# Zero-padded keys and values, so that the score and output matmuls of both attentions use all 128 rows and columns

## The reference

```
# first: 16 query heads, 4 key heads, window keys and context keys side by side
s = concat(einsum(q, k_window), einsum(q, k_context), sink)     # 256 + 256 keys
p = softmax(s * 64 ** -0.5 with band mask)
o = einsum(p, v)                                                # head size 64
# second (256 tokens): 8 heads with three branches, then 8 heads with one
for head in 8 "NSA" heads:   # keys of a group are shared by 4 heads
    o = g0 * attn(q, 15 compressed keys) + g1 * attn(q, k_sel) + g2 * attn(q, k_win)
for head in 8 "MoBA" heads:
    o = attn(q, k, causal)
```

## Time and profile before

| | us |
|---|---|
| median of 3 runs | 2453.49 (2449.99 to 2455.32) |
| the profiled execution | 2460.38 |
| its span, first to last instruction | 2459.1 |
| TensorE busy in the span | 2312.9 (94%) |
| VectorE, ScalarE, GpSimd busy | 1482.0, 1067.9, 120.2 |
| mean granted TensorE clock | 0.936 |

### The profile page before, as it was taken

One profiled execution on the slowest core, in us unless ns is written; L12 is line 12 of the kernel. 1 busy time (PEld: TensorE's weight loads), 2 busy tenths in 40 slices (PEclk: granted clock), 3 DMA queues, 4 the chain that ended last, 5 costly groups with the idle time before them and its releaser, 6 DMA issues. The chain is left out here.

```text
span 2459.1 us, 35571 instructions
## 1 busy us (share of the span) xinstructions
PE 2312.9 (94%) x14610; PEld 2030.3 (83%) x14610; DVE 1482.0 (60%) x2461; ACT 1067.9 (43%) x1740; POOL 120.2 (5%) x83
## 2 busy tenths in 40 slices
PE   5999999999899999999999988969996999999998
PEld 3988889998898888998888985569996975588998
DVE  4765775667566677565677565535654554455555
ACT  4522225644652223563222454554544444334444
POOL 1000001100200000110000020010000010000000
PEclk9999999999899999999999987989997995589999
DMA  6545554455354555444555442014655420034553
GB/s 269 189 159 201 186 162 166 149 194 182 112 184 163 199 181 169 162 158 169 181 198 176 158 159 86 1 52 162 234 187 183 155 103 18 1 102 145 186 174 135
DMA packets 70781, 378.21 MB, mean 154 GB/s; under 512 B 7486, under 2 KB 12478, under 8 KB 43994
## 3 DMA queue, kind: packets, MB, share of 16 engines
q1 hardware_dynamic: 67824, 369.91, 43.5%
q10 hardware_dynamic: 2794, 6.02, 0.7%
HBM read 374.85 MB, written 1.05 MB: 153 GB/s over the span
## 5 line engine op out<-in xcount | busy, mean ns | idle before, releaser
L487 PE MATMUL ps_g<-h,w_hi 128*128 128x256 f32 (+1 forms) x4288 | 1003.9, 329 | 13.7 <-DVE h L930 9.4
L842 DVE TENSOR_TENSOR w_lo<-w_raw,w_hi 128x1024 fp32r<-128x1024 f32 (+2 forms) x614 | 689.1, 1124 | 462.3 <-ACT w_hi L1355 461.6
L1355 ACT ACTIVATE w_hi<-w_raw 128x1024 fp32r<-128x1024 f32 (+2 forms) x614 | 592.6, 969 | 627.7 <-PE ps_g L487 522.2
L487 PEld LDWEIGHTS ps_g<-h,w_hi 128*128 128x128 f32 x4288 | 729.3, 192 | 88.5 <-issue 13.8
L487 PE MATMUL ps_g<-h,w_lo 128*128 128x256 f32 (+1 forms) x2144 | 703.0, 328 | 0.0
L487 PE MATMUL ps_g<-hid,w_hi 128*128 128x256 f32 (+1 forms) x2368 | 497.9, 309 | 3.0 <-DVE y L985 2.0
L487 PEld LDWEIGHTS ps_g<-h,w_lo 128*128 128x128 f32 x2144 | 412.3, 192 | 35.5
L487 PEld LDWEIGHTS ps_g<-hid,w_hi 128*128 128x128 f32 x2368 | 388.0, 193 | 26.4 <-DVE w_lo L842 2.5
L487 PE MATMUL ps_g<-hid,w_lo 128*128 128x256 f32 (+1 forms) x1184 | 364.1, 307 | 0.0
L487 PE MATMUL ps_g<-b_h,w_hi 128*128 128x256 f32 x1504 | 276.8, 287 | 8.1 <-DVE b_h L930 7.8
L487 PEld LDWEIGHTS ps_g<-b_h,w_hi 128*128 128x128 f32 x1504 | 236.8, 193 | 11.4 <-issue 9.9
(11 more groups left out here) (245 smaller groups left out, 1857.1 us busy)
## 6 DMA issues: line engine op xcount, KB each, us to landing
w_raw<-in_gu SPq DMA_DIRECT2D x130, 1024.0 KB, 4.9
mod_raw<-in_w_mod SPq DMA_DIRECT2D x128, 512.0 KB, 3.7
w_raw<-in_conv_cu SPq DMA_DIRECT2D x16, 1024.0 KB, 4.8
w_raw<-in_dn00b SPq DMA_DIRECT2D x16, 768.0 KB, 4.2
w_raw<-in_dn01b SPq DMA_DIRECT2D x16, 768.0 KB, 4.2
w_raw<-in_dn10b SPq DMA_DIRECT2D x16, 768.0 KB, 4.2
w_raw<-in_conv_out SPq DMA_DIRECT2D x8, 1024.0 KB, 4.9
w_raw<-in_w_in_a SPq DMA_DIRECT2D x8, 1024.0 KB, 4.8
```

Of the source, the lines that this page charges most:

```text
L487: mm = pe.matmul(at, w[wp][:, k, m * P:(m + 1) * P], acts[ap][:, k, cs], start=(k == 0 and n == 0 and not (one_bank and m)), stop=(k == kc ...
L842: dve.tensor_tensor(w_lo[u % 2][:, cols], w_raw[u % 2][:, cols], w_hi[u % 2][:, cols].bitcast(F32), ALU.subtract).then_inc(lo_made, 1)
L1355: act.activation(w_hi[u % 2][:, cols], w_raw[u % 2][:, cols], ACT.Copy).then_inc(hi_made, 1)
```

## The change

The keys of each head get a tile of their own, with zeros in the other head's 64 rows; the values of each head get 128 columns, with zeros in the other head's 64. So a score matmul takes all 128 rows of the query tile and an output matmul writes all 128 rows of the result, adding zeros for the other head; the results of a pair of heads now accumulate in one group of matmuls (`first` and `last` are set once for a pair). New is: zeros, written by GpSimd ahead of each attention; the rotations of keys and some copies, done in two halves of 64 rows each; four ScalarE copies that spread the values of `att2`; and semaphores for these.

```diff
-    k1 = yf[:, 8 * S:12 * S].rearrange("p (a n) -> p a n", a=2)
-    m1 = yf[:, 12 * S:14 * S].rearrange("p (a n) -> p a n", a=2)
+    m1 = wide[:].rearrange("p a b n -> p (a b n)")[:, 0:2 * S].rearrange("p (a n) -> p a n", a=2)
+    k1 = yf[:, 8 * S:16 * S].rearrange("p (a n) -> p a n", a=4)
+    v1 = of_hid0[:, :, S:T2]
+    HALF = (slice(0, HD), slice(HD, P))
+    IN_V = (slice(0, HD), slice(S - HD, S))
+    NO_V = slice(HD, S - HD)
...
+    kc2 = small[:, 200:230].rearrange("p (e n) -> p e n", e=2)
+    k2 = yt[:, 0:12, :]
+    v2 = x[:, :, S:T2]
+    v2n = yt[:, 12:16, :]
...
-                    q1[rws, tile, qt * P:(qt + 1) * P], k1[rws, kvh // 2, :], T2, band[:, qt, :],
+                    q1[:, tile, qt * P:(qt + 1) * P], k1[:, kvh, :], T2, band[:, qt, :],
...
-                    [v_tok1[:, kt, kvh * HD:(kvh + 1) * HD] for kt in range(4)],
+                    [v1[:, 2 * kt + kvh // 2, half * P:(half + 1) * P] for kt in range(4)],
...
-                    mm = pe.matmul(ps_s[it.half * HD:(it.half + 1) * HD, a.closed[i] % 2, it.qt * P:(it.qt + 1) * P],
-                                   it.v[k], prod[0:w, i % 2, k * P:(k + 1) * P],
+                    mm = pe.matmul(ps_s[:, a.closed[i] % 2, it.qt * P:(it.qt + 1) * P], it.v[k], prod[0:w, i % 2, k * P:(k + 1) * P],
...
+            pe.wait_ge(zeros1, 3)
             attention(att1)
...
+        pe.wait_ge(zeros2, 6)
+        pe.wait_ge(v2_made, 4)
...
-            dve.tensor_copy(k1[:, :, S:T2], k_raw[:, :, S:T2]).then_inc(rot_made, 1)
+            for e in range(2):
+                ins = dve.tensor_copy(k1[HALF[e], e::2, S:T2], k_raw[HALF[e], :, S:T2])
+            ins.then_inc(rot_made, 1)
...
+                    for e in range(2):
+                        ins = dve.tensor_tensor(k2[HALF[e], 4 * pair - 16 + e:4 * pair - 12:2, :], two[HALF[e], :, :],
+                                                turned[HALF[e], :, :], ALU.add)
...
+                act.activation(v2[:, :, IN_V[e]].rearrange("p (k h) d -> p k h d", k=2),
+                               v_tok2[:, :, S:3 * S].rearrange("p k (h e d) -> p k h e d", e=2, d=HD)[:, :, :, e, :],
+                               ACT.Copy).then_inc(v2_made, 1)
...
+                pool.memset(v1[:, :, NO_V], 0.0).then_inc(zeros1, 1)
...
+                    pool.memset(k1[HALF[1 - e], e::2, :], 0.0).then_inc(zeros1, 1)
...
+        pool.wait_ge(c_first, 2)
+        for n, place in enumerate((k2[HALF[1], 0:12:2, :], k2[HALF[0], 1:12:2, :], v2[:, :, NO_V], v2n[:, :, NO_V],
+                                   v_cmp[:, NO_V], kc2)):
...
+            pool.memset(place, 0.0).then_inc(zeros2, 1)
         pool.wait_ge(r_normed, 14)
```

More of the change, by code:

```diff
@@ L190, in build @@
     apart = ExitStack()
-    sb("skip0", [P, NC, T2], F32, apart)
+    of_hid0 = sb("of_hid0", [P, NC, T2], F32, apart)
     kv_raw = sb("kv_raw", [P, 8 * S], F32, apart)
@@ L308, in build @@
             head = half * 4 + tile
-            rws = slice(half * HD, (half + 1) * HD)
             for qt in range(2):
                 n = (qt + 1) * P
-                qs = qk[rws, tile, qt * P:(qt + 1) * P]
+                qs = qk[:, tile, qt * P:(qt + 1) * P]
                 wgt = [branch[:, qt, 3 * head + b:3 * head + b + 1] for b in range(3)]
[L314 to L320, removed]
+                opens, closes = half == 0 and qt == 0, half == 1 and qt == 1
@@ new lines, in build @@
+                items2.append(Item(qs, kc2[:, half, :], 15, causal[:, S + 15 * qt:S + 15 * qt + 15], None, None, wgt[0],
+                                   [v_cmp[:, half * P:(half + 1) * P]], tile, half, qt, opens, False, opens, False))
+                for b in range(2):
+                    items2.append(Item(qs, k2[:, 8 + 2 * b + half, 0:n], n, causal[:, S - n:S], None, None, wgt[1 + b],
+                                       [v2n[:, 2 * kt + b, half * P:(half + 1) * P] for kt in range(2)],
+                                       tile, half, qt, False, b == 1 and closes, False, b == 1 and closes))
@@ L330, in build @@
+                items2.append(Item(qk[:, 4 + j, qt * P:(qt + 1) * P], k2[:, 2 * j + half, 0:n], n, causal[:, S - n:S],
+                                   None, None, None, [v2[:, 4 * kt + j, half * P:(half + 1) * P] for kt in range(2)],
+                                   4 + j, half, qt, opens, closes, opens, closes))
     Attention = namedtuple("Attention", "items hid b kept closed")
@@ L1034, in rotate1 @@
             dve.wait_ge(rot_step, 2 * rr + 2)
-            dve.tensor_tensor(dst, dst, m1, ALU.add).then_inc(rot_made, 1)
+            if halves is None:
+                ins = dve.tensor_tensor(dst, dst, m1, ALU.add)
+            else:
+                for rows, part in zip(HALF, halves, strict=True):
+                    ins = dve.tensor_tensor(part, src[rows, :, :], m1[rows, :, :], ALU.add)
+            ins.then_inc(rot_made, 1)
         def attention(a):
@@ L1107, in attn_layer @@
                     dve.wait_ge(rope1_in, 16)
-                    rotate1(0, k_raw[:, :, 0:S], k1[:, :, 0:S])
+                    rotate1(0, k_raw[:, :, 0:S], None, [k1[HALF[e], e::2, 0:S] for e in range(2)])
                 if n >= 4:
@@ L1241, in projections @@
             dve.wait_ge(kc_step, 4)
-            dve.tensor_tensor(kc, kc, kc_tmp, ALU.add).then_inc(kc_made, 1)
+            dve.wait_ge(zeros2, 6)
+            for e in range(2):
+                ins = dve.tensor_tensor(kc2[HALF[e], e, :], kc[HALF[e], :], kc_tmp[HALF[e], :], ALU.add)
+            ins.then_inc(kc_made, 1)
         def up_phase():
@@ L1485, in turn_of @@
                 else:
-                    act.activation(v_tok1[:, 2 * s:2 * s + 2, :], ps_g[:, 2 * j + s, :].rearrange("p (a n) -> p a n", a=2),
-                                   ACT.Copy).then_inc(evac, 1)
+                    heads = ps_g[:, 2 * j + s, :].rearrange("p (a e d) -> p a e d", a=4, e=2)
+                    for e in range(2):
+                        ins = act.activation(v1[:, 4 * s:4 * s + 4, IN_V[e]], heads[:, :, e, :], ACT.Copy)
+                    ins.then_inc(evac, 1)
             elif ph == "ple_gate":
```

40 lines of the change are left out of this document (29 added, 11 removed).

## The result

The changed kernel takes 2370.81 us (median of 4 runs, 2370.30 to 2373.59), the kernel before 2454.40 beside it (median of 4): a ratio of 0.9664, 95% interval 0.9652 to 0.9676. One of those four executions of the kernel before took 2575.68 us and is left out of the ratio; the median of the other three is 2453.49. The forecast was 2371.5.

A forecast was written before the change was run, and what follows sets the result against it. TensorE was taken to bound both attentions, through its clock and costs at changes of array shape. Gains 18.9 + 65.5 + 1.9 less costs 4.3 make 82.0 us: 2453.5 - 82.0 = 2371.5 us, own range 2362 to 2382, overall 2358 to 2405.

The forecast's parts named there:

- `att1`, 74.5 forecast: First attention: 69.8 us of bare passes, 2.75 for a half-clock start, 2 for fill and tail; gain 18.9 us.
- `att2`, 68 forecast: Second attention: 63 us at full clock plus 5.5 for a half-clock start, 68 (65 to 73); gain 65.5 us.
- 4 changes of shape each: In `att2`, the 16 compressed items keep odd 15-row and 15-column shapes; their borders cost 10 us.
- 11 us at half clock: Start of `att2`: the clock stays at half for 11 us (5 to 20), costing 5.5 us.
- The entries, 4.3 forecast: Added work ahead of both attentions: 0.35 + 1 + 1.9 + 0.5 + 0.5 us.
- the contention: 1 us (0 to 2.5) for half-adds, copies and zeros ahead of `att1`; 0.5 if zeros slow VectorE ahead of `att2`.
- The zeros' price: GpSimd's 4766 columns of zeros ahead of `att2`: 0 to 11.8 us, hidden in a place of 13.9 us.
- The unit behind `att2`: First projection unit behind `att2`, which had 3.8 us at half clock, gains 1.9 us from a full clock.
- 1 (transposes keep their price): Both attentions: costs at transposes' two borders remain, about 9.5 us in `att1` and 10 in `att2`; 2391 us, chance 0.17.
- 2 (clock down through the NSA heads): `att2`: clock rises only in the MoBA heads, so it takes 101 us instead of 68; 2404 us, chance 0.13.
- 3 (slower): Both attentions: border cost and clock ignore shape and filled rows, so only added costs remain; 2459 us, chance 0.02.
- 4: Both attentions: the clock rises at once and the additions hide, 8 us more gained; 2363 us, chance 0.06.

The follow-up runs named there:

- e1: Keys alone padded, outputs as in the kernel before; one execution, 2383.49 us beside 2454.79 for the kernel before.
- e2: Values alone padded, scores as in the kernel before; one execution, 2444.18 us beside 2454.79 for the kernel before.
- e6: Kernel before plus 24 full-array matmuls on constants in TensorE's wait ahead of `att2`; one execution, 2452.32 us.
- e7: Changed kernel plus full-array matmuls on constants in TensorE's waits, 10 and 12 about `att1`'s last rotation, 33 ahead of `att2`; 2367.35 us, ratio 0.9639.
- e8: Changed kernel with the 16 compressed items transposed and output as whole arrays, added value rows zero; 2369.87 us, ratio 0.9647.
- e9: Kernel before, unpadded, two heads' items side by side, four buffers for turned probabilities, VectorE's low half taken later; 2363.80 us, ratio 0.9633.
- e11: e9 plus full-array matmuls on constants in TensorE's waits, 10 and 12 ahead of `att1`, 24 ahead of `att2`; 2365.38 us, ratio 0.9635.
- e12: e11 with VectorE's split of the second projection weights moved into `att2` and 10 matmuls ahead of it, not 24; 2359.80 us, ratio 0.9614.
- e10: e7 with 16 matmuls ahead of `att2`, plus e8's edit and VectorE's split of the second projection weights moved into `att2`; 2363.83 us, ratio 0.9627.
- e5: Kernel before, unpadded, items in pairs of two heads side by side, two buffers for turned probabilities; 2414.37 us, ratio 0.9814.

## Why the prediction held

*What bounded it: right.* Both causes were real and are now apart: 0.16 us at each border between unlike shapes (e1, e2), and a clock that in `att2` stayed down under 64-row scores (e1 against e2, e6). Why a border costs is not shown: the ends of matmuls are modelled in the trace, so it can't say whether the engine drains there, as I had read it.

*`att1`, 74.5 forecast: 74.2.* The passes were 32 x 2.19 = 70.1 (69.8 forecast). At full clock throughout it is 73.0 (e7), so fill and tail are 2.9 where I had 2, and the half-clock start cost 1.2 where I had 2.75.

*`att2`, 68 forecast: 68.5, with its terms mis-sized.* Three terms were wrong. "4 changes of shape each, at 0.48 / 3 = 0.16, is 10 us": e8 took these borders away and the same work became no shorter, so they set nothing at full clock. "11 us at half clock, cost 5.5": it was 8.9, and cost 2.0 (e7). Against them, at full clock `att2` takes 66.5 and not 63, and PE is busy for only 59.9 of it. I had said that VectorE's and ScalarE's 53 us "fit under it". Their busy time does; but PE waits for their results all the same: it is idle for 6.6 us of e7's `att2`. That 68 met 68.5 was luck in part: the clock's cost was 3.5 too high, the time at full clock 3.5 too low.

*The entries, 4.3 forecast: 2.95.* The copy in halves cost 0.45 (0.35), the key adds with the small one 2.3 and ScalarE's copies some 0.2, 2.5 together (2.4); the contention, 1 us ahead of `att1` and 0.5 for the zeros, didn't show. The zeros' price, bounded by 0 and 11.8, is 4.8. Over all terms the traces give 82.9 us where I had 82.0; the medians differ by 2453.49 - 2370.81 = 82.7.

*The unit behind `att2`:* 1.7 (1.9).

*The rivals.* 1 (transposes keep their price) fell with the item of 2.19 and with e1. 2 (clock down through the NSA heads) fell with the windows; the packed form comes near it, with 42 us of its `att2` at half in e9. The page of the Trainium skill that I had set beside it, "TensorE: Matmul & The Clock Gate", Part 4, on transposes, is neither borne out nor contradicted: no run here takes them away. 3 (slower) needed the border cost to be independent of shape, and e1 and e2 show that it depends on it. 4 was near in its costs; its clock was not at once full.

*What the forecast left out:* that padding is not the cheapest way to rid `att1` of its half-empty array. It had set down the side-by-side outputs of the tail as overlap to be lost, 0.4 to 0.9 us. Made the rule and not the exception, that overlap is worth 13 us of `att1` beyond the padding (60.8 against 74.2, e9).

Open: why the clock stays down in the packed `att2`, whose neighbours fill all rows between them. e9, e11 and e12 don't tell 64-row matmuls in pairs from the shorter time for which they run. Open too: why in `att1` of the kernel before, with 64-row scores of 512 columns, the clock rose after 19 us, and in its `att2` never. Not tried: `att1` packed with `att2` padded. From e12's `att1` (59.9) and e10's total (`att1` 73.0) the estimate is 2363.8 - 13.1 = 2351 us, if the buffers of both forms fit beside each other.

## What to carry to other kernels

Compare the distance between starts with the bare price of a pass at each change of array shape: here 0.16 us, paid three times an item, and making one operand fit removes only one of three. When the clock is low under a busy TensorE, try what the matmuls fill before how densely they come; with two borders left in both, e1's `att2` was 52 us shorter than e2's, most of the 83 that the change gave. And before padding half-filled matmuls, look whether the other half can be given to a neighbour: a padded item of `att1` took 2.19 us, a packed one 1.67, as long as buffers and the engines that copy the results out keep pace and the clock holds.

## What was unexpected in the hardware

- Two matmuls on different halves of the array run fully beside each other in float32: 1.13 us for four passes of 512 columns, against 1.02 for two whole-array passes; sixteen passes of 128 columns in 1.09 us, as long as eight (e9).
- A full clock won by other work was not kept: it was lost 4 us into the unpadded `att2` (e6).
- The clock can alternate. In e5's `att1`, with PE busy for 70 of 89 us, its mean was 0.78: 1.00 from 1530 to 1537 us, 0.66 from 1581 to 1586. In the denser e9 it was 1.00 from 1521 us on.
- A start of `att2` with 8.9 us at half clock cost 2.0 us against a full clock from the start (e7), not 4.5.
